# Expert weights in 2 MB pieces, one 16 KB run per partition, six ring slots instead of twelve

## The reference: what is computed

```python
logits = hf @ w_r + b_r                       # hf (256, 1024), 32 experts
top_val, top_idx = lax.top_k(logits, 4)
top_w = softmax(top_val)
# for each expert e, for the tokens that chose it:
gu  = xe @ w1[e] + b1[e]                      # w1[e] (1024, 2048)
act = (lin + 1) * gate * sigmoid(1.702 * gate)
y  += top_w * (act @ w2[e] + b2[e])           # w2[e] (1024, 1024)
```

## Time and profile before

| | |
|---|---|
| median of three runs | 1304.34 us (1302.7 to 1309.38) |
| span of the profiled execution, first to last instruction | 1304.7 us |
| PE busy | 1176.4 us, 90% |
| read from HBM | 446.7 MB |

### The profile page before, as it was taken

How to read it: one execution, slowest core, us unless ns; L and a number is a source line. 1 busy time by engine, 2 the same in 40 slices (tenths; PEclk the granted TensorE clock), 3 DMA queues, 4 the chain that set the end, 5 groups by cost and what they waited for, 6 DMA issues and landing times. The chain is left out here.

```text
span 1304.7 us, 16649 instructions
## 1 busy us (share of the span) xinstructions
PE 1176.4 (90%) x6368; PEld 467.0 (36%) x6368; DVE 281.4 (22%) x787; ACT 211.7 (16%) x430; POOL 34.1 (3%) x49
## 2 busy tenths in 40 slices
PE   7999999989999988888888888888888888888868
PEld 4455544454433322333333322222333333322223
DVE  1474533372211111111111111111111111111121
ACT  2223445021111111111111111111111111111110
POOL 2221100000000000000000000000000000000000
PEclk9999999988999999999999999999999999999989
DMA  9835041962999999999999999999999999999930
GB/s 290 287 129 193 3 128 72 376 264 121 402 418 418 418 417 417 417 417 418 418 418 418 418 418 418 418 417 417 416 418 417 418 418 418 418 418 418 418 160 32
DMA packets 95555, 448.08 MB, mean 343 GB/s; under 512 B 12821, under 2 KB 15230, under 8 KB 62670
## 3 DMA queue, kind: packets, MB, share of 16 engines
q1 hardware_dynamic: 94078, 442.25, 84.3%
q0 software_dynamic: 1264, 5.27, 1.2%
q10 hardware_dynamic: 192, 0.29, 0.1%
HBM read 446.71 MB, written 4.22 MB: 346 GB/s over the span
## 5 line engine op out<-in xcount | busy, mean ns | idle before, releaser
L330 PE MATMUL ps<-ring,wbuf 128*64 128x512 f32 x2048 | 481.5, 603 | 74.2 <-DMA ring<-in_w_e 74.2
L330 PEld LDWEIGHTS ps<-ring,wbuf 128*64 128x64 f32 x2048 | 133.1, 137 | 404.7 <-DMA ring<-in_w_e 223.4
L354 PE MATMUL ps<-ring,wbuf 128*64 128x512 f32 x1024 | 226.8, 596 | 21.6 <-ACT wbuf L369 21.6
L403 DVE TENSOR_SCALAR wbuf<-ps 128x512 f32<-128x512 f32 x32 | 22.1, 692 | 769.1 <-PE ps L330 769.1
L354 PEld LDWEIGHTS ps<-ring,wbuf 128*64 128x64 f32 x1024 | 70.7, 137 | 157.1 <-issue 127.9
L365 ACT ACTIVATE wbuf<-wbuf 128x512 f32<-128x512 f32 x32 | 20.1, 629 | 536.0 <-DVE wbuf L403 536.0
L1088 PE MATMUL ps<-wbuf,hT 128*128 128x512 f32 (+2 forms) x224 | 87.1, 549 | 1.0 <-ACT hT L562 1.0
L317 PE MATMUL ps<-wbuf 64*128 64x512 f32 x264 | 65.6, 615 | 0.7 <-ACT wbuf L371 0.7
L1170 PE MATMUL ps<-wbuf,hT 128*128 128x512 f32 x128 | 62.0, 613 | 0.0
L1088 PEld LDWEIGHTS ps<-wbuf,hT 128*128 128x128 f32 x224 | 43.2, 195 | 41.8 <-issue 38.8
L371 ACT COPY wbuf<-ps 128x512 f32<-128x512 f32 x32 | 18.7, 585 | 230.0 <-PE ps L354 230.0
(11 more groups left out here) (231 smaller groups left out, 691.2 us busy)
## 6 DMA issues: line engine op xcount, KB each, us to landing
ring<-in_w_e SPq DMA_DIRECT2D x384, 1024.0 KB, 22.2
wbuf<-in_w_in SPq DMA_DIRECT2D x9, 2048.0 KB, 9.1
wbuf<-in_w_out SPq DMA_DIRECT2D x1, 4096.0 KB, 14.2
rel_rows_repeated<-rel_rows POOLq DMA_DIRECT2D x1, 3072.0 KB, 19.1
wbuf<-in_w_ple_gate SPq DMA_DIRECT2D x1, 3072.0 KB, 17.1
ring<-rel_rows_repeated POOLq DMA_DIRECT2D x1, 2048.0 KB, 11.9
wbuf<-in_w_branch_a SPq DMA_DIRECT2D x2, 1024.0 KB, 9.9
wbuf<-in_w_branch_b SPq DMA_DIRECT2D x1, 2048.0 KB, 17.6
```

The lines of the kernel that those rows point to most:

```text
L330: l = mm((G, Lb)[n // 2][(n % 2) * SLOTS:(n % 2 + 1) * SLOTS, :], xeT[:, k, :], ring3[:, k, n * 512:(n + 1) * 512], start=False, stop=k == ...
L354: l = mm(O[n * SLOTS:(n + 1) * SLOTS, :], actT[:, kt % 4, (kt // 4) * SLOTS:(kt // 4 + 1) * SLOTS], ring3[:, i, r * DM + n * 512:r * DM + ...
L403: d.tensor_scalar(gc, ps[0][:, :], LIMIT, None, ALU.min).then_inc(s["gc_ready"], 1)
```

## The change

Six slots of 2 MB take the place of twelve of 1 MB, in the same memory. Piece i of w1 is rows 256i to 256i+255, two consecutive rows in each partition, one run of 16 KB. Piece h of w2 is rows 512h to 512h+511, four consecutive rows in each partition, also one run of 16 KB. Where TensorE picks columns for the matching operand, it now takes every second one (`rows_of`, for the gather and for `x_rows`) or every fourth one (`act`). The router's weights and the FFN gain get the same order; the gain is loaded by itself as four rows of 256 and turned by two small transposes whose results are interleaved. One piece is released when both (w1) or all four (w2) of its slices have been used. The initial loads are the same regions at the same points of SyncE's order.

```diff
-PIECES = 12
-UP = 8
+PIECES = 6
+UP = 4
+RUN = 2
+RUN2 = 4
-        w1 = io["w_e1"][0].rearrange("e (k p) n -> e k p n", p=P)
-        w2 = io["w_e2"][0].rearrange("e (q r p) n -> e q p r n", r=2, p=P)
+        w1 = io["w_e1"][0].rearrange("e (q p r) n -> e q p r n", p=P, r=RUN)
+        w2 = io["w_e2"][0].rearrange("e (h p r) n -> e h p r n", p=P, r=RUN2)
             if i < UP:
-                eng.dma_start(ring3[:, i, :], w1[e, i]).then_inc(signal[i], 16)
+                eng.dma_start(ring3[:, i, :].rearrange("p (r n) -> p r n", r=RUN), w1[e, i]).then_inc(signal[i], 16)
             else:
-                eng.dma_start(ring3[:, i, :].rearrange("p (r n) -> p r n", r=2), w2[e, i - UP]).then_inc(signal[i], 16)
+                eng.dma_start(ring3[:, i, :].rearrange("p (r n) -> p r n", r=RUN2), w2[e, i - UP]).then_inc(signal[i], 16)
+        def rows_of(k):
+            at = (k // RUN) * RUN * P + k % RUN
+            return slice(at, at + RUN * P - RUN + 1, RUN)
...
-                            l = mm(O[:, k * SLOTS:(k + 1) * SLOTS], hp[:, q, t, k * P:(k + 1) * P], S[:, t, :],
+                            l = mm(O[:, k * SLOTS:(k + 1) * SLOTS], hp[:, q, t, rows_of(k)], S[:, t, :],
...
-                for k in range(UP):
-                    te.wait_ge(a["piece"][k], it * 16 + 16)
-                    for n in range(4):
-                        l = mm((G, Lb)[n // 2][(n % 2) * SLOTS:(n % 2 + 1) * SLOTS, :], xeT[:, k, :], ring3[:, k, n * 512:(n + 1) * 512],
-                               start=False, stop=k == UP - 1)
+                for i in range(UP):
+                    te.wait_ge(a["piece"][i], it * 16 + 16)
+                    for r in range(RUN):
+                        k = RUN * i + r
+                        for n in range(4):
+                            l = mm((G, Lb)[n // 2][(n % 2) * SLOTS:(n % 2 + 1) * SLOTS, :], xeT[:, k, :],
+                                   ring3[:, i, r * 2 * DFF + n * 512:r * 2 * DFF + (n + 1) * 512], start=False, stop=k == KT - 1)
                     l.then_inc(s["pieces_used"], 1)
...
-                    l = tr(T[:, j * P:(j + 1) * P], act[:, j * P:(j + 1) * P], ident)
+                    l = tr(T[:, j * P:(j + 1) * P], act[:, j:512:RUN2], ident)
...
-                    for r in range(2):
-                        kt = 2 * (i - UP) + r
+                    for r in range(RUN2):
+                        h = i - UP
                         for n in range(2):
-                            l = mm(O[n * SLOTS:(n + 1) * SLOTS, :], actT[:, kt % 4, (kt // 4) * SLOTS:(kt // 4 + 1) * SLOTS],
+                            l = mm(O[n * SLOTS:(n + 1) * SLOTS, :], actT[:, r, h * SLOTS:(h + 1) * SLOTS],
...
-                for i in range(8):
+                for i in range(4):
                     load(sp, 0, i, piece)
                 sp.wait_ge(pr_used, 4)
...
-                load(sp, 0, 8, piece)
-                load(sp, 0, 9, piece)
+                load(sp, 0, 4, piece)
...
-                for i in range(10, PIECES):
-                    load(sp, 0, i, piece)
+                load(sp, 0, 5, piece)
...
-                        l = tr(b[:, 0:24], grow, ident[0:24, 0:24])
+                        tr(b[:, 0:16], grow, ident[0:16, 0:16])
+                        for r in range(RUN):
+                            l = tr(b[:, 16 + r:24:RUN], gffn[:, r:RUN * P:RUN], ident[0:KT // RUN, 0:KT // RUN])
...
-                        l = tr(b[:, i * P:(i + 1) * P], src[:, t, (k0 + i) * P:(k0 + i + 1) * P], ident)
+                        l = tr(b[:, i * P:(i + 1) * P], src[:, t, cols(k0 + i)], ident)
```

More of the change, by code:

```diff
@@ L99, in sem @@
             return ctx.enter_context(nc.semaphore(name))
-        ring = sb("ring", PIECES * 2048)
+        ring = sb("ring", PIECES * 4096)
         wbuf = sb("wbuf", 4 * 4096)
@@ L192, in block_kernel @@
         pe_in = g0(2, P, parts=16)
-        grow = g0(P, parts=24)
+        grow = g0(P, parts=16)
+        gffn = g0(RUN * P, parts=KT // RUN)
         tab, onehot, erow = g0(16, parts=BUCKETS + 1), g0(384, parts=BUCKETS + 1), g0(384, parts=16)
@@ L350, in expert_pe @@
                     te.wait_ge(a["piece"][i], it * 16 + 16)
-                    for r in range(2):
-                        kt = 2 * (i - UP) + r
+                    for r in range(RUN2):
+                        h = i - UP
                         for n in range(2):
-                            l = mm(O[n * SLOTS:(n + 1) * SLOTS, :], actT[:, kt % 4, (kt // 4) * SLOTS:(kt // 4 + 1) * SLOTS],
-                                   ring3[:, i, r * DM + n * 512:r * DM + (n + 1) * 512], start=kt == 0, stop=kt == 7)
+                            l = mm(O[n * SLOTS:(n + 1) * SLOTS, :], actT[:, r, h * SLOTS:(h + 1) * SLOTS],
+                                   ring3[:, i, r * DM + n * 512:r * DM + (n + 1) * 512], start=h == 0 and r == 0, stop=h == 1 and r == RUN2 - 1)
                     l.then_inc(s["pieces_used"], 1)
@@ L382, in take_rows @@
             def take_rows():
-                d.tensor_tensor(xeT, ps[2][:, :].rearrange("p (k c) -> p k c", k=KT), bc(gT[:, 8:16], SLOTS), ALU.mult).then_inc(s["xe_ready"], 1)
+                d.tensor_tensor(xeT, ps[2][:, :].rearrange("p (k c) -> p k c", k=KT), bc(gT[:, 16:24], SLOTS), ALU.mult).then_inc(s["xe_ready"], 1)
             ve.wait_ge(hp_ready, 4)
@@ L438, in _ @@
                             sp.dma_start(ck2w[:, i, :], io[n][0]).then_inc(ld_small, 16)
-                        sp.dma_start(wr, io["w_router"][0].rearrange("(k p) n -> p k n", p=P)).then_inc(ld_route, 16)
+                        sp.dma_start(wr.rearrange("p (q r) n -> p q r n", r=RUN), io["w_router"][0].rearrange("(q p r) n -> p q r n", p=P, r=RUN)).then_inc(ld_route, 16)
                         sp.dma_start(br, io["b_router"].to_broadcast([P, NE])).then_inc(ld_route, 16)
@@ L546, in _ @@
                 sc.dma_start(const_all, cst).then_inc(ld_const, 16)
-                for i, n in enumerate(("g_mix", "g_ffn", "g_ple")):
+                for i, n in enumerate(("g_mix", "g_ple")):
                     sc.dma_start(grow[i * 8:(i + 1) * 8, :], io[n][0].rearrange("(k p) -> k p", p=P)).then_inc(ld_const, 16)
+                sc.dma_start(gffn, io["g_ffn"][0].rearrange("(q c) -> q c", c=RUN * P)).then_inc(ld_const, 16)
                 def tjob(name):
@@ L711, in _ @@
                         l = a.activation(hTv[:, k0 + i, t * P:(t + 1) * P], ps[4 + k % 2][:, i * P:(i + 1) * P], ACT.Copy,
-                                         scale=gT[:, 8 + k0 + i:9 + k0 + i])
+                                         scale=gT[:, 16 + k0 + i:17 + k0 + i])
                     l.then_inc(t_ev, 1)
@@ L1202, in branch, with half_rows @@
                     l.then_inc(pr_ps, 1)
-                def half_rows(src, n, at):
+                def half_rows(src, n, at, cols):
                     b = tbank(NT + at)
@@ L1213, in merged_rows @@
                     te.wait_ge(pr_used, n + 1)
-                    half_rows(merged, n, n)
+                    half_rows(merged, n, n, lambda k: slice(k * P, (k + 1) * P))
                 def w_out(i):
@@ L1225, in x_rows @@
                     te.wait_ge(x2_ready, n + 1)
-                    half_rows(x, n, 4 + n)
+                    half_rows(x, n, 4 + n, rows_of)
                 def router(t):
@@ L1344, in _ @@
                         kk = 2 * n + i
-                        l = a.activation(x3T[:, kk, :], ps[n % 2][:, i * SEQ:(i + 1) * SEQ], ACT.Copy, scale=gT[:, 16 + kk:17 + kk])
+                        l = a.activation(x3T[:, kk, :], ps[n % 2][:, i * SEQ:(i + 1) * SEQ], ACT.Copy, scale=gT[:, 8 + kk:9 + kk])
                     l.then_inc(p_ev, 1)
```

## The result

| | before | after |
|---|---|---|
| median | 1304.47 us (1302.70 to 1309.38, 4 runs) | 1289.07 us (1282.65 to 1290.73, 4 runs) |
| ratio to before | | 0.9858, interval 0.9836 to 0.9880 |
| span of the profiled execution | 1304.7 us | 1287.1 us |

A forecast was written before the change was run, and what follows sets the result against it. The prediction took the expert loop to be bound by the weight stream. Its terms, -22.5 + 1.5 + 1.7 + 0.3 + 0.2 = -18.8 us, took 1304.7 to 1285.9 us, median 1285.5, range 1276 to 1303.

The forecast's parts named there:

- The stream: Expert loop's weight loads: fixed 9.4 ns a packet, so 16 KB runs make a visit 29.34 us; gain 22.5 us.
- rival 1: Weight loads: runs over 8 KB bring nothing, everything moves at 422.5 GB/s; 1299 us; chance 0.20.
- rival 3: Weight loads: the new order of reads is slower in HBM, at 410 GB/s; 1325 us; chance 0.06.
- rival 4: Weight loads: more gain than forecast, by a cost per DMA; 1272 to 1280 us; chance 0.04.
- The hole: Weight loads at 336 to 342 us, 307 GB/s: 1.6 us lost before, half taken as gone.
- Coarser ends: Both ends of the weight loads: first reload 2.3 us later, net cost 1.5 us; last w1 piece 1.7 us longer.
- the gains' three transposes: Before the x transposes: one transpose becomes three, 0.2 us at most, all on the path.
- Strided operands: TensorE's strided reads: no change for gather and x_rows; activation transposes, if doubled, cost 0.3 us at the end.
- rival 2: Gather loses its overlap through strided columns and TensorE becomes the bound; 1338 us; chance 0.10.
- The clock: TensorE's granted clock, 1.00 in the loop: taken as unchanged; nothing put for the stretch behind the last scatter.
- The sum: Whole kernel: -18.8 us on the profiled execution, 1304.7 to 1285.9 us; median 1285.5 us, 1.4% faster.

The follow-up runs named there:

- the first experiment: Changed kernel with its six 2 MB slots, but rows dealt as before (8 KB and 4 KB runs, contiguous operands), against the kernel before: 1309.69 us, ratio 1.0019.

## Why the prediction was right

*The stream.* The step that carries the forecast held: a fixed cost for each packet, worked out from two rates, gave 29.34 us for 16 KB (29.37 measured), 29.8 for w2 in 8 KB (29.81), 30.7 for all in 4 KB (30.72) and 29.21 for w1 in 32 KB (29.21). One number, 9.4 ns, covers five periods. (In the reading of the earlier trace rows slice 11 stands at 402 GB/s and not at 416 to 418, and PE falls to 8 only from slice 15; the period comes from the later visits and isn't touched.) Of the Trainium skill, "DMA: Bandwidth & Descriptors", section "Why small descriptors are slow (HBM only)", the kind of cost agrees with the runs, the size does not: by an estimate from its 3 cycles a packet the period would be near 29.8 us, and the measurement decides.

*No cost of a DMA, no cut runs, no slower reads from HBM.* Short runs in big pieces gave 30.12 us; the packet counts are those of whole runs of 16 and 32 KB; nothing fell under its worked-out rate. Rivals 1, 3 and 4 fall.

*The hole.* I had read it as 1.6 us lost in the kernel before and taken half of it as gone, because the stream starts later. It was a matter of that one execution. The kernel before with eight matmuls in its last block runs the same loop, and its window has no hole:

```profile
336.00:342.00 6.00, 6.00 (x34) 2.08 (x32) 0.00 (x0) 1.87 (x2) 0.00 (x0) 1.00 1.02 410
```

There the first reload comes at 313.62 us and the last w1 piece's first matmul at 1241.13, 927.5 us later, against the 928.0 of the table. So the hole cost 0.5 us and not 1.6; the DMA share of the earlier trace rows, 0.91 where full windows have 1.02, gives 0.7 us as well. The stretch of the table shrank by 23.6 us: 22.8 by the two periods over 30 visits and one w1, 0.5 by the hole, 0.3 left over. The 0.8 that the sum had for it came close by luck.

*Coarser ends.* The last w1 piece: 1.72 us longer, as forecast. At the start 2.3 + 0.2 us was forecast and 2.1 measured, but that is luck too. TensorE's clock was near 0.50 at the first w1 matmuls in both profiles. The kernel with w2 in one run (twelve slots) and the changed kernel run again have 1.00 there (window 310 to 315 us). Their first w1 matmul and first reload:

```profile
310.89 11.33 PE L330 MATMUL ps<-ring,wbuf 128*64 128x512 f32 x52
...
312.98 12.33 SPq L294 DMA_DIRECT2D ring<-in_w_e  x8
```
```profile
310.96 13.90 PE L340 MATMUL ps<-ring,wbuf 128*64 128x512 f32 x64
...
314.76 10.62 SPq L297 DMA_DIRECT2D ring<-in_w_e  x4
```

That is 2.09 us with 1 MB pieces and 3.80 with 2 MB, so the coarser piece costs 1.7 us at the start as at the end, and not 2.3. In the pair of this document it is 315.20 - 311.38 = 3.8 against 317.26 - 312.03 = 5.2 us, 1.4 us, and the other 0.7 of the 2.1 us lies ahead of the first w1 matmul. Of that, the gains' three transposes have 0.2, as forecast: the x transposes start at 7.27 instead of 7.08 us. The whole of the coarser ends is measured by the ratio of 1.0019 in the first experiment, 2.5 us (0.4 to 4.6), against 3.4 by the terms of the sum (1.5, 1.7 and 0.2).

*Strided operands.* The gather went from 1.58 to 1.60 us, so rival 2 falls; with 8 B between columns it takes 1.76. The transposes of the activation went from 0.63 to 0.72 us, 0.1 instead of the 0.3 I had put, and the slack hides it in all visits but the last. They take 0.72 us with a step of 8 B too, in the kernel with w2 in one run (next row), and 0.63 in the first experiment, where they are contiguous. The Trainium skill's rule in "SBUF — State Buffer", section "Door 1: The DMA port swizzle", that a second hit in a 16 B line keeps the full rate, would have 8 B free and 16 B not; the runs show the same small cost for both. By the same rule bf16 columns 8 B apart would be free, and the gather takes 1.76 us with them. The Trainium skill's rule in "TensorE: Matmul & The Clock Gate", section "Weight-path perf modes", that the fast load takes strided columns, agrees with the 1.60 us.

```profile
1236.80 0.72 PE L345 MATMUL ps<-misc,wbuf 128*128 128x128 f32 x4
```

*The clock.* Here a term was missing. In the loop I had it right: 1.00. Behind the loop I had put no difference, and this profile has 2.1 us, because after the same idleness of 7.6 to 7.7 us the clock came back later, some 4 us into the last group and not ahead of it. It doesn't follow the run length, the stride or the slots: without additional matmuls at the end the last group took 27.73 us with short runs in big pieces, with 4 KB packets and with runs of 32 KB, and 29.93 us with w2 in one run of 8 KB. But it belongs to this comparison more than chance would have it. Three of three profiles of the changed kernel have the longer form, and of its 14 recorded executions 9 have a mean clock over the span of 0.984, where 6 of 47 of the kernel before are at 0.984 or less. That mean takes in both ends of the kernel and so does not say which stretch it was, and the kernel before has one profile alone. What decides between the two forms stays open; only that the clock is what differs is shown, by the additional matmuls.

*The sum.* -18.8 us was forecast for the span, and -17.6 measured. Of the 1.2 us between them the tail gives 2.1; against it stand 0.4 at the first reload, 0.3 in the stretch of the stream and 0.2 at the transposes. The mean spans of the 14 and the 47 executions, 1286.44 and 1304.18 us, lie 17.7 us apart, so the pair's two peculiarities, the hole and the tail, did not make the result.

## What to carry to other kernels

Where the DMA engines are busy all the time, look at the rate by part of the loop, not at its mean: two parts with different run lengths give the fixed cost of a packet and so the worth of a longer run, before anything is built. Dealing the contraction rows to partitions in consecutive rows costs nothing in the stream here and almost nothing at TensorE (0.1 us a visit). Where the consumer has slack, what a coarser piece costs is its own additional time at each end of the stream, here 1.7 us at either end for 2 MB, which is why 32 KB brought no more than 16.

## What was not expected

The same kernel's clock differs from one execution to the next outside the loop: three profiles of the changed kernel have spans of 1287.1, 1285.0 and 1287.3 us, and its runs go from 1282.65 to 1291.88 us while its loop's period repeats to 0.01 us. The hole in the stream of the kernel before was such a thing too, and I had put it into a sum. A few microseconds at either end of this kernel are such a chance, and a gain of that size needs more than one profile. In the loop with 4 MB pieces the clock fell in single stretches behind waits such as the one of 2.62 us, and cost the loop nothing, as the stream was the bound: the mean rate stayed at 431 GB/s and the mean period at the 29.21 us worked out.
